# Delta-rule stage of a two-block kernel: gates' chain and small inverse in two parts, key tiles in banks 0 to 2, one gate for two head pairs

## Chip, cores, metric

One core of one Trainium2 chip runs the whole program in one launch. The metric is the device time in microseconds (us), the median of three runs. Six engines' queues matter: TensorE (PE; its weight loads are listed as PEld), VectorE (DVE), ScalarE (ACT), GpSimd (POOL, which only fills constants here), SyncE (SP), whose queue issues every DMA, and the DMA engines themselves. TensorE runs at one of two clocks, 1.2 or 2.4 GHz; the profile gives the granted clock as a share, 0.50 or 1.00.

## What is computed

A tensor x of 256 tokens by 1024 channels goes through a first block (convolution and pooling mixer, then a gated feed-forward part), and then through two layers: a gated delta rule, and a block attention, each with a layer norm and a SwiGLU feed-forward part. The change touches the delta rule alone, with 8 heads of 128 keys and 128 values, cut to what matters:

```python
proj = x @ w_in                                    # q, k, v, z, b, a
qkv = silu(causal_depthwise_conv(qkv, w_conv))     # 4 taps
q, k = l2_normalize(q) * 128 ** -0.5, l2_normalize(k)
beta = sigmoid(b)
g = -exp(a_log) * softplus(a + dt_bias)
gc = cumsum(g)                                     # within a chunk
low = strict_tril((k * beta) @ k.T * decay)        # decay = exp(gc_i - gc_j)
u, w = solve(I + low, [v * beta, k * beta * exp(gc)])
v_new = u - w @ state
o = (q * exp(gc)) @ state + tril(q @ k.T * decay) @ v_new
state = state * exp(gc_last) + k_dec.T @ v_new
o = o * rsqrt(mean(o * o) + eps) * norm_g * silu(z)
y = o @ w_out
```

The kernel works with two chunks of 128 tokens (index c) and handles the heads in halves (q = 0, 1: four heads) or in pairs (u = 0 to 3).

## The kernel before

**Matmuls.** Every product with a weight is made of three float32r matmuls, `three` (L489): high part of the weight by high and low part of the data, low part by high part. A weight unit is a 128 by 1024 block. ScalarE makes its high part (`high`, L962), VectorE its low part (`low`, L1422), four units ahead of TensorE.

**The order.** `delta_order` (L123) is written out by hand and called by TensorE, ScalarE and VectorE alike, each with its own functions; every engine runs its share in that order and waits on semaphores. A function named "nothing" means that the engine has no part in the step. Steps are:

- `tile(n)`: key tiles n = 0 to 7, value tiles 8 to 15, query tiles 16 to 23, 24 matmuls each on TensorE, in two halves. ScalarE then scales the last tap (L1210, out of the bank), VectorE adds three taps (L1732) and ScalarE's silu (L1200) follows in the next tile. Tiles use banks 4 to 6 in turn.
- `ba`, `gsum`, `rows`, `decays`: the gates. TensorE makes b and a (bank 7); ScalarE and VectorE make beta and g (L1159 to L1164, L1693 to L1703, ending in gg); TensorE sums g (`gsum`, L705); VectorE copies the sums (gcol, L1710); `rows(c, q)` (L715) spreads them along rows, ScalarE takes them out (L1172 and L1176 or L1179), VectorE caps them (L1716); `decays` takes exponentials (L1184 to L1195).
- `kturn(q)` turns four heads' keys (ScalarE squares them, L1217, takes a root, L1220, VectorE scales, L1748), `kback(q)` turns them back (ScalarE copies, L1227 and L1232), `kk(q)` multiplies keys by keys (L671; VectorE makes low of it in crow, L1767), `lowT(q)` turns low.
- `z(k)`: the eight z units, into all of banks 4 to 7; ScalarE's silu of them (L1154) is at k = 7.
- `inv(q)`: VectorE inverts the 16 by 16 blocks on the diagonal in 15 rounds (L1786, L1789). The blocks come and go by SP's DMAs: low out and in (L447, L451), the inverse out and back into tm (L454, L461). `turnT(q)` turns that, then `level_p` and `level_t` double the block size by products.
- `vturn`, `solve`, `state`, `carry`: values, the solve, the state between chunks.
- `qk(u)`, `attnT(u)`, `o(u)`, `gate(u)`, `gturn(u)`: attention within the chunk (L818), its turn (L833), the output (L841, L848), its norm with z (VectorE L1866 to L1877, ScalarE L1297 and L1300), its turn (L856). `qk(u)` also sums q squares (L824, squares from ScalarE, L1282, in crow).
- `gout(k)`: eight units of w_out.

**Banks.** Small steps take banks 0 to 3 in a ring (`Ring`, L110, `take_bank`): the fifth taker waits until the event that the first named has passed. Semaphores count, in each engine's own order.

Of the kernel before, what the change touches and what calls it, by code (L numbers as in the profile page):

```python
# [13 lines left out]
P = 128  # L14
# [108 lines left out]
def delta_order(do):  # L123
# [81 lines left out]
    do["gturn"](2)  # L205
    do["gout"](2)
    do["o"](3)
    do["gate"](3)
# [77 lines left out]
def program(nc, wts, head, vecs, csts, xtok, xT, low_dram, inv_dram, out):  # L286
    with ExitStack() as ctx:
# [90 lines left out]
        pba = bank[7][:, 0:32].rearrange("p (c n) -> p c n", c=2)  # L378
# [104 lines left out]
        def tensor(g, s):  # L483
# [178 lines left out]
            core_bank = Ring({b: ("hl", ("x2", 0)) for b in range(4)})  # L662
# [17 lines left out]
            def z(k):  # L680
# [1437 lines left out]
```

## Time and profile before

| | us |
|---|---|
| median of 3 runs | 1186.29 (1185.02 to 1186.57) |
| profiled execution, its own time | 1184.9 |
| its span, first to last instruction | 1183.1 |
| mean granted clock of TensorE | 0.982 |

The page of the profile gives the busy time of each engine as a share of the span, the chain of work that ended last, and the costliest groups of instructions. TensorE's busy time is an average over stages; in the delta-rule stage, from 422.6 to 643.9 us of the span, it is 196.12 of 221.3 us. A bracket at the end of a row of the timeline is the idle time of that engine before the row and the instruction that ended it. Matmuls overlap, so a row's start, not its duration, tells when the next could begin.

### The profile page before, as it was taken

Reading aid. Unit: us, or ns where it says so; the run is one execution under the profiler, and the core shown is the slowest. Engines: PE = TensorE matmul, PEld = TensorE weight load, DVE = VectorE, ACT = ScalarE, POOL = GpSimd, SP = SyncE. Lnnn points to the kernel's source line nnn. Section 1 sums busy time; section 2 is a strip of 40 time slices with the busy share of each in tenths; the row PEclk is TensorE's granted clock in tenths of the full one; section 3 lists DMA queues with packets and bytes.
Section 4 is the critical chain, followed back from the end, with each engine's and each line's share of the span. In section 5 each row is a group of like instructions: output and inputs, shape, how many; then the busy total and the mean of one; then the engine's idle time right before and its main releaser. Section 6 shows DMA issues by size and latency. Waiting matters only on the chain.

```text
span 1183.1 us, 21225 instructions
## 1 busy us (share of the span) xinstructions
PE 1124.9 (95%) x8872; PEld 1094.1 (92%) x8872; DVE 811.5 (69%) x1364; ACT 619.9 (52%) x1037; POOL 3.3 (0%) x13
## 2 busy tenths in 40 slices
PE   7998989999999996979989999999999999999998
PEld 7998878899999985879989999999999899999997
DVE  7987479878887776585666755555688557555554
ACT  5567454555466567633463554544455446544442
POOL 0000000000000000000000000000000000000000
PEclk9999999999999997989989999999999999999999
DMA  9985247267766512233223365656346335555500
GB/s 372 409 327 168 72 143 285 89 197 236 253 203 202 193 54 93 70 101 130 90 71 127 107 205 186 196 182 194 108 161 195 108 107 158 186 191 186 189 2 36
DMA packets 58127, 194.71 MB, mean 165 GB/s; under 512 B 10800, under 2 KB 11184, under 8 KB 57904
## 3 DMA queue, kind: packets, MB, share of 16 engines
q1 hardware_dynamic: 58032, 193.35, 48.9%
q8 instruction: 70, 1.15, 0.4%
q14 instruction: 25, 0.20, 0.1%
HBM read 192.02 MB, written 1.31 MB: 163 GB/s over the span
## 4 chain that ended last, share of the span: by engine, by line
PE 74%; DVE 17%; ACT 6%; issue 2%; SPq 1%; DMA 0%; POOL 0%; ACTq 0%; DVEq 0%; POOLq 0%
PE ps L492 61%; DVE lo L1422 4%; PE ps L671 3%; ACT hi L962 2%; PE ps L499 2%; DVE raw L1409 2%; PE ps L590 2%; DVE B L1431 1%; PE ps L511 1%; DVE st L1439 1%; DVE ev L1660 1%; DVE B L1444 1%; DVE B L1732 1%; PE ps L487 1%; DVE ev L1657 1%
## 5 line engine op out<-in xcount | busy, mean ns | idle before, releaser
L492 PE MATMUL ps<-hh,hi 128*128 128x256 f32 x1792 | 509.8, 285 | 15.6 <-DVE hl L1456 3.5
L492 PE MATMUL ps<-hl,hi 128*128 128x256 f32 x1792 | 503.2, 281 | 0.0
L492 PE MATMUL ps<-hh,lo 128*128 128x256 f32 x1792 | 503.0, 281 | 0.0
L1422 DVE TENSOR_TENSOR lo<-raw,hi 128x1024 fp32r<-128x1024 f32 x311 | 378.1, 1222 | 175.4 <-ACT hi L962 174.7
L492 PEld LDWEIGHTS ps<-hh,hi 128*128 128x128 f32 x1792 | 340.2, 190 | 19.3 <-issue 8.9
L962 ACT ACTIVATE hi<-raw 128x1024 fp32r<-128x1024 f32 x311 | 324.4, 1052 | 50.4 <-PE ps L492 50.3
L492 PEld LDWEIGHTS ps<-hl,hi 128*128 128x128 f32 x1792 | 340.1, 190 | 0.3
L492 PEld LDWEIGHTS ps<-hh,lo 128*128 128x128 f32 x1792 | 340.0, 190 | 0.0
L492 PE MATMUL ps<-fh,hi 128*128 128x256 f32 x568 | 159.4, 281 | 2.9 <-ACT B L1066 2.9
L492 PE MATMUL ps<-fh,lo 128*128 128x256 f32 x568 | 158.5, 279 | 0.0
L492 PE MATMUL ps<-fl,hi 128*128 128x256 f32 x568 | 158.4, 279 | 0.0
L492 PEld LDWEIGHTS ps<-fh,hi 128*128 128x128 f32 x568 | 106.8, 188 | 3.5 <-ACT B L1066 3.5
L492 PEld LDWEIGHTS ps<-fl,hi 128*128 128x128 f32 x568 | 106.8, 188 | 0.0
L492 PEld LDWEIGHTS ps<-fh,lo 128*128 128x128 f32 x568 | 106.8, 188 | 0.0
L1123 ACT ACTIVATE ev<-ps 128x256 f32<-128x256 f32 x88 | 33.7, 383 | 121.4 <-PE ps L492 121.4
L487 PE MATMUL ps<-idle 128*128 128x256 f32 x456 | 62.2, 294 | 1.7 <-POOL Z L477 1.7
L487 PEld LDWEIGHTS ps<-idle 128*128 128x128 f32 x456 | 58.4, 196 | 2.6 <-POOL Z L477 1.7
L1409 DVE CUSTOM_DVE_ANT_0 raw<-raw,crow 128x1024 f32<-128x1024 f32 x48 | 58.3, 1218 | 0.0
L1667 DVE TENSOR_TENSOR ev<-ev 128x256 f32<-128x256 f32 x66 | 28.0, 425 | 37.4 <-ACT ev L1123 26.8
L1669 DVE TENSOR_TENSOR fl<-ev,fh 128x256 fp32r<-128x256 f32 x66 | 28.1, 426 | 32.0 <-ACT fh L1127 32.0
L1732 DVE SCALAR_TENSOR_TENSOR B<-ps,vec,B 128x255 f32<-128x255 f32 (+2 forms) x72 | 34.6, 481 | 18.6 <-ACT B L1210 16.9
L1127 ACT ACTIVATE fh<-ev 128x256 fp32r<-128x256 f32 x66 | 27.6, 419 | 37.6 <-DVE ev L1667 37.6
(242 smaller groups left out, 1096.5 us busy)
## 6 DMA issues: line engine op xcount, KB each, us to landing
raw<-in_w SPq DMA_DIRECT2D x359, 512.0 KB, 4.1
B<-in_t SPq DMA_DIRECT2D x2, 512.0 KB, 5.5
xa<-in_x SPq DMA_DIRECT2D x1, 1024.0 KB, 11.6
out<-h SPq DMA_DIRECT2D x2, 512.0 KB, 2.9
cst<-in_c SPq DMA_DIRECT2D x1, 984.0 KB, 9.4
B<-between SPq DMA_DIRECT2D x32, 4.0 KB, 1.6
vec<-in_v SPq DMA_DIRECT2D x1, 328.5 KB, 7.3
between<-crow SPq DMA_DIRECT2D x16, 8.0 KB, 1.5
```

Of the source, the lines that this page charges most:

```text
L487: g.matmul(bank[7][:, 0:S], idle[:, 0:P], idle[:, :], start=True, stop=True, skip_group_check=True)
L492: m = g.matmul(o, l, r, start=first and n == 0, stop=last and n == 2, skip_group_check=True)
L499: m = g.matmul(bank[bm][:, 0:S], ones[:, one, :], y[:, k, :], start=k == 0, stop=k == nch - 1, skip_group_check=True)
L671: m = g.matmul(bank[b][:, i * P:i * P + P], left(i), right(i), start=i == 0, stop=True, skip_group_check=True)
L962: g.activation(hi[:, j % SPLIT, :], raw[:, PLACE[j] % RAW, :], ACT.Copy).then_inc(*up("hi", j))
L1123: g.activation(e, p, ACT.Copy if half else ACT.Silu).then_inc(*up("ff_out", (kup, t)))
L1127: g.activation(fh[:, j % 4, :], ev[:, (2 * j) % 4, :], ACT.Copy).then_inc(*up("f_hi", (kup, j)))
L1409: g.tensor_tensor_reduce(r, r, crow[:, :], 1.0, 0.0, ALU.mult, ALU.add, mod[:, col:col + 1]).then_inc(*up("ada", n))
L1422: g.tensor_tensor(lo[:, j % SPLIT, :], raw[:, PLACE[j] % RAW, :], hi[:, j % SPLIT, :].bitcast(F), ALU.subtract).then_inc(*up("lo", j))
L1667: g.tensor_tensor(e0, e0, e1, ALU.mult).then_inc(*up("f", (kup, j)))
L1669: g.tensor_tensor(fl[:, j % 4, :], e0, fh[:, j % 4, :].bitcast(F), ALU.subtract).then_inc(*up("f_lo", (kup, j)))
L1732: m = g.scalar_tensor_tensor(out=dst[:, d:], in0=bank[b][:, 0:S - d], scalar=V("a_conv", t * 4 + i), in1=dst[:, d:], op0=ALU.mult, op1=ALU ...
```

## The change

It writes `delta_order` in another way and adapts the functions to it:

1. Key tiles 0 to 7 use banks 0 to 2 (`tile_bank`), b and a and the sums bank 3, and rows(0, 0) and rows(0, 1) banks 6 and 7. z(0) waits for rows(0, 1) alone, and not for the last key tiles; the ring's banks wait for the last key tiles instead.
2. The gates' chain is in two parts, `soft(0)` after tile 3 and `soft(1)` after tile 4; gsum comes after tile 5, rows(0, 0) after tile 6, rows(0, 1) and kturn(0) after tile 7, rows(1, q) and decays after z(0), kback(0) after z(1).
3. inv(1) is in two parts, six rounds after tile 8 and nine after tile 9. ScalarE's silu of z takes the banks in the order 2, 0, 1, 3.
4. The q sums move from qk(u) to attnT(u), in bank 7 (a ring bank for u = 3).
5. gate(0) and gate(1) become one step with one root and one reciprocal, after tile 22; o, qk, attnT, gturn and gout are in another order from tile 19 on.

```diff
     for n in range(8):
         tile(n)
         if n == 2:
             do["ba"]()
+        elif n == 3:
+            do["soft"](0)
         elif n == 4:
+            do["soft"](1)
+        elif n == 5:
             do["gsum"]()
+        elif n == 6:
             do["rows"](0, 0)
+        elif n == 7:
             do["rows"](0, 1)
-        elif n == 5:
-            do["rows"](1, 0)
-            do["rows"](1, 1)
-        elif n == 6:
             do["kturn"](0)
     for k in range(8):
         do["z"](k)
         if k == 0:
+            do["rows"](1, 0)
+            do["rows"](1, 1)
             do["decays"]()
+        elif k == 1:
             do["kback"](0)
-        elif k == 1:
             do["kturn"](1)
...
         elif k == 6:
-            do["inv"](0)
+            do["inv"](0, 0, 15)
     tile(8)
-    do["inv"](1)
+    do["inv"](1, 0, 6)
     tile(9)
+    do["inv"](1, 6, 15)
...
-    tile(19, [then("qk", 0)], [then("attnT", 0), then("state", 1)])
-    tile(20, [then("o", 0), then("carry", 1)], [then("gate", 0)])
-    tile(21, [then("qk", 1), then("solve", 3)], [then("attnT", 1), then("gturn", 0)])
-    tile(22, [then("o", 1)], [then("gate", 1)])
-    tile(23, [then("qk", 2), then("gturn", 1)], [then("attnT", 2)])
+    tile(19, [then("qk", 0)], [then("state", 1)])
+    tile(20, [then("attnT", 0), then("carry", 1)], [then("qk", 1)])
+    tile(21, [then("o", 0), then("solve", 3)], [then("attnT", 1)])
+    tile(22, [then("o", 1)], [then("gate", 0, 1)])
+    tile(23, [then("qk", 2)], [then("gturn", 0), then("gturn", 1), then("attnT", 2)])
     do["last"]()
+    do["gout"](0)
+    do["qk"](3)
     do["o"](2)
-    do["gout"](0)
-    do["gate"](2)
-    do["qk"](3)
     do["gout"](1)
     do["attnT"](3)
-    do["gturn"](2)
+    do["gate"](2)
     do["gout"](2)
     do["o"](3)
+    do["gturn"](2)
     do["gate"](3)
...
+        def tile_bank(n):
+            return n % 3 if n < 8 else 4 + n % 3
...
-            core_bank = Ring({b: ("hl", ("x2", 0)) for b in range(4)})
+            core_bank = Ring({0: ("conv4", 6), 1: ("conv4", 7), 2: ("conv4", 5), 3: ("gcum", 0)})
...
                 if k == 0:
-                    for n in (5, 6, 7):
-                        s.wait_ge(*at("conv4", n))
-                    s.wait_ge(*at("gcum"))
+                    s.wait_ge(*at("rows_out", (0, 1)))
...
-                b = take_bank("rows_out", (c, q))
+                b = take_bank("rows_out", (c, q)) if c else 6 + q
...
+                b = take_bank("qss", 3) if u == 3 else 7
+                if u < 3:
+                    s.wait_ge(*(at("qss", u - 1) if u else at("z", 3)))
+                s.wait_ge(*at("qsq", u))
...
-                        [at("conv4", n) for n in (21, 22, 23)] + [at("z", 3)] if k == 0 else [])
+                        [at("conv4", n) for n in (21, 22, 23)] + [at("qss", 2)] if k == 0 else [])
...
-                    for b in range(4):
+                    for b in (2, 0, 1, 3):
```

The order of instructions shows what this does to the queues. First ScalarE from the tap of tile 2 on (sm holds the gates, hi a weight's high part, B keys; L1200 and L1159 to L1164 before are L1210 and L1168 to L1174 after). Before:

```order
L1210 ACTIVATE B<-ps,vec 128x256
L1159 ACT_TABLE_LOAD
L1159 ACTIVATE sm<-ps 128x16
L1160 ACT_TABLE_LOAD
L1160 ACTIVATE sm<-vec 128x8
L1162 ACTIVATE sm<-sm 128x16
L1164 ACT_TABLE_LOAD
L1164 ACTIVATE sm<-sm 128x16
L962 ACTIVATE hi<-raw 128x1024
```

Now, from the second operation of soft(0) on (the Exp of a_log):

```order
L1169 ACTIVATE sm<-vec 128x8
L1171 ACTIVATE sm<-sm 128x16
L970 ACTIVATE hi<-raw 128x1024
L1210 ACT_TABLE_LOAD
L1210 ACTIVATE B<-B 128x256
L1220 ACTIVATE B<-ps,vec 128x256
L1174 ACT_TABLE_LOAD
L1174 ACTIVATE sm<-sm 128x16
L970 ACTIVATE hi<-raw 128x1024
```

A high part, a Silu load, a silu and a tap stand between the two halves of the chain.

Second, ScalarE around z(0) and z(1) (Z holds rows and decays; the last two rows before are kback(0)'s copies). Before:

```order
L1200 ACTIVATE B<-B 128x256
L1184 ACT_TABLE_LOAD
L1184 ACTIVATE sm<-sm 128x16
L1186 ACTIVATE sm<-sm 128x8
L1191 ACTIVATE Z<-Z 128x512 x4
L1195 ACTIVATE Z<-Z 128x512 x2
L1227 ACTIVATE Z<-B,sm 128x128 x4
L1232 ACTIVATE B<-ps 128x4x128 x2
```

Now:

```order
L1189 ACTIVATE Z<-ps 128x512
L1194 ACT_TABLE_LOAD
L1194 ACTIVATE sm<-sm 128x16
L1196 ACTIVATE sm<-sm 128x8
L1201 ACTIVATE Z<-Z 128x512 x4
L1205 ACTIVATE Z<-Z 128x512 x2
L970 ACTIVATE hi<-raw 128x1024
L1237 ACTIVATE Z<-B,sm 128x128 x4
L1242 ACTIVATE B<-ps 128x4x128 x2
```

The rows of the second chunk now stand right ahead of the decays, and a high part between the decays and the copies.

Third, VectorE at the gate behind tile 22 (sm holds sums and factors, the products write og in B; the first row is the last tap of tile 22). Before, gate(1) alone:

```order
L1732 SCALAR_TENSOR_TENSOR B<-ps,vec,B 128x253
L1866 TENSOR_REDUCE sm<-B 128x2x2
L1869 SCALAR_TENSOR_TENSOR sm<-sm 128x2x2
L1872 RECIPROCAL sm<-sm 128x2x2
L1877 SCALAR_TENSOR_TENSOR B<-ps,sm,B 128x128 x4
L1422 TENSOR_TENSOR lo<-raw,hi 128x1024
```

Now, gate(0, 1):

```order
L1747 SCALAR_TENSOR_TENSOR B<-ps,vec,B 128x253
L1883 TENSOR_REDUCE sm<-B 128x2x2
L1886 SCALAR_TENSOR_TENSOR sm<-sm 128x2x2
L1883 TENSOR_REDUCE sm<-B 128x2x2
L1886 SCALAR_TENSOR_TENSOR sm<-sm 128x2x2
L1890 RECIPROCAL sm<-sm 128x2x4
L1896 SCALAR_TENSOR_TENSOR B<-ps,sm,B 128x128 x8
L1434 TENSOR_TENSOR lo<-raw,hi 128x1024
```

The products of both pairs stand behind both sums and one common reciprocal.

## Rows read from the trace of the kernel before

**Rows 1.** The page, busy time of each engine: us, share of the span, instructions.

```profile
PE 1124.9 (95%) x8872; PEld 1094.1 (92%) x8872; DVE 811.5 (69%) x1364; ACT 619.9 (52%) x1037; POOL 3.3 (0%) x13
```

**Rows 2.** Timeline, TensorE in the stage: start, us, engine, line, operation [idle before, releaser].

```profile
442.67 0.61 PE L705 MATMUL ps<-sm,cst 128*128 128x8 f32 x4 [1.16 <-DVE sm L1703]
449.48 3.78 PE L715 MATMUL ps<-cst,sm 128*128 128x128 f32 x16 [6.20 <-DVE sm L1710]
...
470.71 0.77 PE L492 MATMUL ps<-hi,hh 128*128 128x512 f32 x1 [5.71 <-DVE B L1732]
...
482.89 1.95 PE L671 MATMUL ps<-B 128*128 128x128 f32 x16
...
504.89 0.39 PE L492 MATMUL ps<-hh,hi 128*128 128x256 f32 x1 [1.66 <-ACT B L1154]
...
518.35 1.54 PE L677 MATMUL ps<-first,B 128*128 128x128 f32 x6 [4.70 <-DMA B<-between]
...
595.34 1.05 PE L824 MATMUL ps<-ones,crow 128*128 128x1 f32 x8 [2.32 <-ACT crow L1282]
...
608.43 1.87 PE L824 MATMUL ps<-ones,crow 128*128 128x1 f32 x8 [2.32 <-ACT crow L1282]
```

**Rows 3.** Stretches of the stage: us, PE busy (instructions), granted clock, DMA share, GB/s.

```profile
444.30:454.60 10.30, 5.12 (x24) 0.50 0.31 102
468.20:475.10 6.90, 4.39 (x11) 0.51 0.47 156
516.00:522.80 6.80, 4.45 (x21) 0.50 0.56 167
608.20:615.00 6.80, 6.57 (x31) 0.50 0.25 78
```

**Rows 4.** Timeline, ScalarE between tiles 2 and 4.

```profile
440.69 1.28 ACT L1164 ACT_TABLE_LOAD   x1
441.98 0.21 ACT L1164 ACTIVATE sm<-sm 128x16 f32<-128x16 f32 x1
442.10 1.04 ACT L962 ACTIVATE hi<-raw 128x1024 fp32r<-128x1024 f32 x1
...
444.45 0.42 ACT L1200 ACTIVATE B<-B 128x256 f32<-128x256 f32 x1
444.78 0.46 ACT L1210 ACTIVATE B<-ps,vec 128x256 f32<-128x256 f32 x1
```

**Rows 5.** Timeline, VectorE: the three taps of tile 2, and the copy gcol.

```profile
437.78 1.51 DVE L1732 SCALAR_TENSOR_TENSOR B<-ps,vec,B 128x255 f32<-128x255 f32 x3
...
449.26 0.17 DVE L1710 COPY sm<-ps 128x16 f32<-128x16 f32 x1
```

**Rows 6.** Timeline, ScalarE: rows(1, 0), decays, and kback(0)'s copies.

```profile
457.66 1.15 ACT L1172 ACTIVATE Z<-ps,sm 128x128 f32<-128x128 f32 x4 [0.42 <-PE ps L715]
...
472.54 2.17 ACT L1191 ACTIVATE Z<-Z 128x512 f32<-128x512 f32 x4
...
475.67 1.26 ACT L1227 ACTIVATE Z<-B,sm 128x128 f32<-128x128 f32 x4
476.83 1.06 ACT L1232 ACTIVATE B<-ps 128x512 f32<-128x512 f32 x2
```

**Rows 7.** Timeline, VectorE: both products into crow, inv(0)'s first row, the row behind it.

```profile
485.16 2.15 DVE L1767 SCALAR_TENSOR_TENSOR crow<-ps,sm,Z 128x128 f32<-128x128 f32 x8
...
494.22 2.16 DVE L1767 SCALAR_TENSOR_TENSOR crow<-ps,sm,Z 128x128 f32<-128x128 f32 x8 [1.84 <-DMA between<-crow]
...
500.44 0.28 DVE L1780 COPY blk<-cst 64x256 f32<-64x256 f32 x1
...
507.72 2.34 DVE L1422 TENSOR_TENSOR lo<-raw,hi 128x1024 fp32r<-128x1024 f32 x2
```

**Rows 8.** Timeline, VectorE at gate(0): the sum of squares and the four products.

```profile
592.71 0.68 DVE L1866 TENSOR_REDUCE sm<-B 128x4 f32<-128x512 f32 x1
...
594.07 1.12 DVE L1877 SCALAR_TENSOR_TENSOR B<-ps,sm,B 128x128 f32<-128x128 f32 x4
```

More of the change, by code:

```diff
@@ L820, in qk @@
                 m.then_inc(*up("qk", u))
-                b = take_bank("qss", u)
-                s.wait_ge(*at("qsq", u))
-                for n in range(4):
-                    m = g.matmul(bank[b][:, n:n + 1], qsq[:, u % 2, n % 2, n // 2 * P:n // 2 * P + P], ones[:, 2, 0:1],
-                                 start=n == 0, stop=True, skip_group_check=True)
-                m.then_inc(*up("qss_mm", u))
             def attnT(u):
@@ L834, in attnT @@
                 m.then_inc(*up("attnT_mm", u))
+                b = take_bank("qss", 3) if u == 3 else 7
+                if u < 3:
+                    s.wait_ge(*(at("qss", u - 1) if u else at("z", 3)))
+                s.wait_ge(*at("qsq", u))
+                for n in range(4):
+                    m = g.matmul(bank[b][:, n:n + 1], qsq[:, u % 2, n % 2, n // 2 * P:n // 2 * P + P], ones[:, 2, 0:1],
+                                 start=n == 0, stop=True, skip_group_check=True)
+                m.then_inc(*up("qss_mm", u))
             def o(u):
@@ L861, in gout @@
                 rows_in("gout", k, 4, xh[:, k, :], xl[:, k, :], at("gl", k // 2), k == 0, k == 7,
-                        [at("conv4", n) for n in (21, 22, 23)] + [at("z", 3)] if k == 0 else [])
+                        [at("conv4", n) for n in (21, 22, 23)] + [at("qss", 2)] if k == 0 else [])
             def nothing(*a):
                 pass
-            delta_order({"z": z, "ba": ba, "gsum": gsum, "rows": rows, "decays": nothing, "tile": gdn_tile, "kturn": kturn,
+            delta_order({"z": z, "ba": ba, "soft": nothing, "gsum": gsum, "rows": rows, "decays": nothing, "tile": gdn_tile, "kturn": kturn,
                          "kback": kback, "kk": kk, "lowT": lowT, "inv": nothing, "turnT": turnT, "level_p": level_p, "level_t": level_t, "vturn": vturn,
@@ L1293, in o, with gate @@
                 o_bank[u] = take_bank()
-            def gate(u):
-                s.wait_ge(*at("o_mm", u))
-                g.activation(two(tm, u), by_two(o_bank[u]), ACT.Square).then_inc(*up("osq", u))
-                v = mo[:, :, 2 * u:2 * u + 2]
-                s.wait_ge(*at("orms", u))
-                g.activation(v, v, ACT.Sqrt).then_inc(*up("osd", u))
+            def gate(*us):
+                for u in us:
+                    s.wait_ge(*at("o_mm", u))
+                    g.activation(two(tm, u), by_two(o_bank[u]), ACT.Square).then_inc(*up("osq", u))
+                v = mo[:, :, 2 * us[0]:2 * us[-1] + 2]
+                s.wait_ge(*at("orms", us[-1]))
+                g.activation(v, v, ACT.Sqrt).then_inc(*up("osd", us[-1]))
             def gturn(u):
@@ L1315, in nothing @@
                 pass
-            delta_order({"z": z, "ba": ba, "gsum": nothing, "rows": rows, "decays": decays, "tile": gdn_tile, "kturn": kturn,
+            delta_order({"z": z, "ba": nothing, "soft": soft, "gsum": nothing, "rows": rows, "decays": decays, "tile": gdn_tile, "kturn": kturn,
                          "kback": kback, "kk": kk, "lowT": lowT, "inv": nothing, "turnT": turnT, "level_p": level_p, "level_t": level_t, "vturn": vturn,
@@ L1727, in gdn_tile @@
                     return
[L1728 removed]
+                dst, b = (kb, vb, qb)[n // 8][:, n % 8, :], tile_bank(n)
                 s.wait_ge(*at("conv4_0", n))
@@ L1774, in lowT, with inv @@
                 take_bank()
-            def inv(q):
+            def inv(q, j0, j1):
                 a, x = bm[q]
-                g.tensor_copy(x, C("eye16")[0:64, :].rearrange("p (i j) -> p i j", i=16)).then_inc(*up("inv", (q, 0)))
-                s.wait_ge(s_blk[q], 16)
-                for j in range(15):
+                if j0 == 0:
+                    g.tensor_copy(x, C("eye16")[0:64, :].rearrange("p (i j) -> p i j", i=16)).then_inc(*up("inv", (q, 0)))
+                    s.wait_ge(s_blk[q], 16)
+                for j in range(j0, j1):
                     n = 15 - j
@@ L1894, in nothing @@
                 pass
-            delta_order({"z": z, "ba": ba, "gsum": gsum, "rows": rows, "decays": decays, "tile": gdn_tile, "kturn": kturn,
+            delta_order({"z": z, "ba": nothing, "soft": soft, "gsum": gsum, "rows": rows, "decays": decays, "tile": gdn_tile, "kturn": kturn,
                          "kback": kback, "kk": kk, "lowT": lowT, "inv": inv, "turnT": turnT, "level_p": level_p, "level_t": level_t, "vturn": one_bank,
```

116 lines of the change are left out of this document (62 added, 54 removed).

## The prediction, on record before the changed kernel ran

> **What bounds it.** I read the page first: TensorE is busy 95% of the span [rows 1], so time can only come from the moments in which it waits or runs slowly. Next I read TensorE's timeline through the delta-rule stage (422.6 to 643.9) and looked only at rows with a bracket, which give the idle time and its releaser. There are seven long ones [rows 2]: 1.16 and 6.20 us in the gates' chain (for VectorE's gg, then its copy gcol), 5.71 before z(0) (for the taps of tile 7, because z takes the tiles' banks), 1.66 before tile 8 (for the third z activation on ScalarE), 4.70 before turnT(0) (for the small inverse coming back by DMA), and twice 2.32 at the q sums (for ScalarE's square into crow). Together 24.1 us. Third, the busy time by stretch: in four stretches the granted clock is 0.50, the lower level (1.2 GHz), and they hold 5.12 + 4.39 + 4.45 + 6.57 = 20.5 us of TensorE work [rows 3]. At the upper level that work takes half as long, so 10.3 us are lost there. Each stretch begins some 2 to 3 us into a wait (two adjoining waits in the first) and ends 4 to 7 us after work resumes; the waits of 1.66 and the first 2.32 drew none. The stage thus holds 34 us to be had. Last I read ScalarE's and VectorE's timelines, to see what each wait becomes once the order changes.
>
> **The change, part by part.** I carry one clock, the profile's, and put each engine's queue through the new order. A key tile costs TensorE about 2.85 us: three tiles lie between 504.89 and 513.65, where the wait for turnT(0) begins [rows 2].
>
> *Gates' chain.* Until tile 3 nothing moves. VectorE ends tile 2's taps at 439.3 [rows 5] and ScalarE its silu of it at 439.7. Now ScalarE does: tile 3's tap 0.4, Sigmoid load and beta 1.5, Exp load with two exps 1.6, a weight's high part 0.95, Silu load and silu 1.7, tap 0.4, Ln load and Ln 1.5 [rows 4]. That is 8.1 us, to 447.8; two small VectorE operations later gg stands at 448.2, not at 442.6. TensorE has tile 5 as new cover and ends it at 444.3 (441.5, the start of the 1.16 wait [rows 2], plus 2.8). It waits 4.0 us there. Then gsum 0.5 and tile 6, to 451.6. Meanwhile ScalarE needs high part, Silu load, silu and tap (3.1 us, to 450.9), VectorE three taps and the copy of gcol (1.5 + 0.2 [rows 5]): gcol stands at 452.5, so rows(0,0) waits 0.9. Rows(0,0) 1.0 (it and rows(0,1) took 3.78 at the lower clock [rows 2], so 1.9 at the upper) and tile 7 take TensorE to 456.4; rows(0,1) and one turn cover 1.4 us of tile 7's tap and taps, and the second turn, in bank 1, waits 1.3 for them. z(0) starts at 459.5. The 4.0 us wait should draw the lower clock; part of that hides under the waits behind it, and I add 0.5 between 0 and 2.6 (half of the mean 5.13 us of [rows 3]). So 460.0 instead of 470.71 [rows 2]. Of these 10.7 us, 1.8 are only postponed, since rows(1,0) and rows(1,1), which ran ahead of z(0), now follow it: 8.9 us ahead.
>
> *What is late next: ScalarE.* It was ahead of TensorE; now it isn't. Its last square of the first key turn ends at 460.8. Behind it, without a pause, stand Sqrt load and root 1.6, high part 0.95, Silu load and silu 1.7, rows(1,0) and rows(1,1) at 1.6 each (four activations 1.15 and a copy of 0.5, half the pair in the last row), Exp load and two small exps 1.6, six decays 3.2 (four take 2.17), high part 0.95, the four scaled copies 1.2 and the pair of copies 1.0 [rows 6]: 15.3 us, to 476.1. kk(0) needs that pair. TensorE has z(0) to z(2) at 2.8 each (twelve matmuls of 512 columns, a key tile's 24 of 256), the rows 1.9 and two pairs of turns at 0.8 as cover and is there at 471.9: **a new wait of 4.2 us**. kk(0) at 476.1 instead of 482.89 [rows 2] leaves 6.8 us. From there the chain goes on: squares, Sqrt load, high part (3.6 us, ScalarE at 479.7), VectorE's low part 1.2 and the products into crow 2.15, which end at 483.2 instead of 487.3 [rows 7]. The second products start 6.9 us later in both, since they wait for the DMAs of the first [rows 7], and end at 492.3 instead of 496.4. inv(0) follows 4.1 us after that in the profile, partly at TensorE's pace of z(5); behind VectorE alone I make it 3.5. inv(0) starts at 495.8 instead of 500.44: 4.6 us ahead. inv(0)'s 7.3 us and the 10.6 us from its end (507.8) to turnT(0) at 518.35 stay as they are [rows 2, 7]. So **turnT(0) comes 4.5 us earlier**, at 513.8, after a wait of about 6 us instead of 4.7. Bounds: 8.9, if ScalarE's queue does not hold kk(0), and 2.5, if the lower clock takes 2.6 before z(0).
>
> *z's activations in another order* release tile 8 about 1.0 us sooner (two activations of 0.5). It saves nothing: turnT(0), 8.6 us behind, waits for the DMA anyway. *inv(1) in two parts*: 9 of its 15 rounds (4.2 of 7.3 us) now stand behind tile 9's low part and taps, 2.7 us. TensorE asks for it two tiles and ten products behind turnT(0), some 15 us (kk's pair of products takes 1.95 [rows 2]), and no wait stands there now; I cost the split at nothing, and that stretch is its cover. VectorE does the same work between inv(0) and the first level product, so that does not move either.
>
> *The q sums and the joint gate.* The q sums move behind attnT, so both 2.32 us waits go [rows 2]. But bank order matters: from o(0), the fourth bank taken after its own is qk(2)'s, and o(0)'s bank is released by the gated product, which now comes from gate(0,1) for both pairs. ScalarE can square only after tile 22's tap, VectorE does tile 22's taps 1.5, then two reductions of 0.68 [rows 8], each with a small sum behind it (0.9 together), root and reciprocal 0.5, four products 1.12 [rows 8]: from tile 22's end on TensorE to the release 5.4 us, of which half a tile covers 1.4. **qk(2) waits 4.0 us**. Every wait of that length in [rows 2] drew the lower clock, so 2.6 more. Then gout(0) needs qss(2) on VectorE behind tile 23's taps and two gl: 1.6 us. Sum 8.2, against 2 x 2.32 + 6.57 / 2 = 7.9 before [rows 2, 3]: 0.3 us worse. Bounds: 2.4 us better with no lower clock, 2 worse with it held through gout(0).
>
> *Table loads.* Each takes 1.28 us and the activation starts 0.02 us behind it [rows 4]. One more stands in the gates' chain (Silu between Exp and Ln), one Sqrt load fewer at the joint gate; both are in the sums. The Trainium skill, "ScalarE: Activation LUTs", section "Table sets: the hidden batching unit", speaks against the split: activations are to be batched by set, and "What ACT_TABLE_LOAD costs" puts a switch at 2.66 us with its drain. By that price the five switches up to gcol would cost 6.9 us more and the lead would be gone (my estimate); the trace does not agree, it shows 1.28 and no drain behind it, so the measurement decides, and as a rival (1186, no change) it keeps no chance.
>
> **Sum.** 4.5 - 0.3 = 4.2 us. The profiled execution took 1184.9 (span 1183.1), 1.4 below the median of the three runs, 1186.3. 1180.7 in its terms, **1182.0 us** in the median's. A measurement of this kernel can tell about 0.2%, 2.4 us, from no change.
>
> **Rivals.** *All of the lead is kept* (ScalarE's queue holds less than I say, and the joint gate draws no lower clock): 8.9 + 2.4 = 11.3 us, 1175. For it: over the span ScalarE is busy only 52% of the time [rows 1]. Against: those 15.3 us are a plain queue. *The lead is given back at the second inverse*: inv(1) ends 2.7 us later behind inv(0), and its DMAs share SP's queue with the weights; if they land so late that turnT(1) waits 2 us and the clock falls (2.6 more), 4.6 are gone: 1186.5, no change. Against: the 15 us of tiles and products between. *Slower, by the clock*: the new order has four long waits as before (4.0, 4.2, 6, 4.0) and six short ones (0.6 to 1.6) close behind them. The first stretch of [rows 3] shows two adjoining waits holding the lower clock for 10.3 us. If the short ones do that everywhere, half-clocked work doubles to 41 us, which costs 10.3 more: 1192. It decides from 13 us more of such work (6.6 us lost). Against: after the wait of 5.71 the clock was back within 4.4 us of work. *The change doesn't do what it says*: for the split inverse and z's order that is my forecast already; for the gates, gg comes 5.6 us later, only the cover grows.
>
> **Chances.** My forecast 0.58, with its own range 1178.5 to 1185.5, of which 0.50 lies below 1183.9; all kept 0.13; given back 0.18 (0.05 faster, 0.13 same); slower 0.11. Faster 0.68, same 0.21, slower 0.11. The range 1176.5 to 1186.5 leaves out about half of the first rival, the whole slower case and a little of the third.
>
> **What would show it.** Right: in the changed profile TensorE waits about 4 us for VectorE at gsum, 1 to 1.5 at the second key turn, 3 to 5 for ScalarE's copies at kk(0), about 6 for the DMA at turnT(0), 4 for VectorE at qk(2), 1 to 2 at gout(0), none for crow; z(0) starts near 460, turnT(0) near 514. Wrong: no wait at kk(0) (then the first rival), a wait at turnT(1) (the second), more than 33 us of work at 0.50 (the third).

## The result, and the profile after

The changed kernel takes 1179.15 us in the median of 12 runs (1176.67 to 1182.92), the kernel before, in 12 runs beside them, 1186.05 us (1182.84 to 1188.83). The ratio is 0.9949 with a 95% interval of 0.9935 to 0.9962: 6.0 us faster by the ratio, 4.5 to 7.7 (the two medians lie 6.9 apart). The forecast was 4.2 us and 1182.0; 1179.15 lies at the lower end of its range (1178.5 to 1185.5). The profiled execution took 1179.46 (span 1177.7), 5.4 less than that of before (1184.9).

The page's busy time, which answers to [rows 1]: the same 8,872 matmuls, 3.7 us less of TensorE, VectorE and ScalarE unchanged. So work has not gone; waits and slow stretches have.

```profile
PE 1121.2 (95%) x8872; PEld 1090.4 (93%) x8872; DVE 811.3 (69%) x1363; ACT 620.0 (53%) x1035; POOL 3.3 (0%) x13
```

TensorE's timeline in the stage, the rows with a bracket, as in [rows 2]. The stage starts 0.65 us later than before (first tile's second step at 426.41 against 425.76), so 0.65 is to be taken off when a start is held against one of before.

```profile
448.93 1.02 PE L711 MATMUL ps<-sm,cst 128*128 128x8 f32 x4 [3.96 <-DVE sm L1717]
...
461.29 0.65 PE L685 MATMUL ps<-first,B 128*128 128x128 f32 x4 [0.99 <-DVE B L1747]
...
477.31 2.05 PE L679 MATMUL ps<-B 128*128 128x128 f32 x16 [3.44 <-ACT B L1242]
...
484.10 0.66 PE L685 MATMUL ps<-first,crow 128*128 128x128 f32 x4 [1.07 <-DVE crow L1782]
...
500.33 0.39 PE L500 MATMUL ps<-hh,hi 128*128 128x256 f32 x1 [0.69 <-ACT B L1162]
...
514.74 1.97 PE L685 MATMUL ps<-first,B 128*128 128x128 f32 x8 [5.73 <-DMA B<-between]
...
602.76 2.08 PE L824 MATMUL ps<-B 128*128 128x128 f32 x8 [3.94 <-DVE B L1896]
...
611.11 0.36 PE L500 MATMUL ps<-fh,hi 128*128 128x256 f32 x1 [0.88 <-DVE sm L1870]
```

The waits of 6.20 (rows), 5.71 (z(0)) and twice 2.32 (crow) are gone. New are 3.44 at kk(0) and 3.94 at qk(2), the wait at gsum grew from 1.16 to 3.96, that at turnT(0) from 4.70 to 5.73. In sum (with a second wait of 0.37 behind that of 1.07) 24.1 us of waiting became 21.1, so waiting explains 3.0 us. Most of the rest is the clock, in the stretches that answer to [rows 3] (from the third column on: busy time and instructions of PE, PEld, VectorE, ScalarE and GpSimd, then clock, DMA share and GB/s):

```profile
448.40:455.20 6.80, 6.28 (x29) 6.28 (x30) 4.31 (x9) 4.42 (x7) 0.00 (x0) 0.50 0.29 94
513.20:520.00 6.80, 5.26 (x25) 5.27 (x26) 6.15 (x23) 2.92 (x5) 0.00 (x0) 0.50 0.43 114
602.00:608.80 6.80, 6.04 (x28) 6.04 (x29) 4.71 (x12) 3.46 (x6) 0.00 (x0) 0.50 0.23 78
```

Three stretches at 0.50 (1.2 GHz) instead of four, with 17.6 us of work instead of 20.5; half of the difference, 1.5 us, is gained. The new wait at kk(0) drew none: from 475.0 to 500.0 the clock is 1.00. Together that is 4.5 of the 4.7 us by which the stage is shorter in these two profiles (224.8 and 220.1 us, the sums of the two columns of the table below).

ScalarE's timeline between its last square of the first key turn and the copies that kk(0) needs. Nothing in between has a bracket: one queue of 15.1 us (462.6 to 477.7).

```profile
461.98 0.60 ACT L1227 ACTIVATE h<-ps 128x512 f32<-128x512 f32 x1 [0.21 <-PE ps L685]
...
471.44 2.18 ACT L1201 ACTIVATE Z<-Z 128x512 f32<-128x512 f32 x4
...
475.51 1.26 ACT L1237 ACTIVATE Z<-B,sm 128x128 f32<-128x128 f32 x4
476.68 1.06 ACT L1242 ACTIVATE B<-ps 128x512 f32<-128x512 f32 x2
```

VectorE's timeline from the second key turn to the first small inverse, and then that of SyncE's queue from its end on. The inverse ends at 504.2; its result goes out in one DMA and comes back in 16, which take 7.35 us to issue; turnT(0) follows 1.2 us behind the last.

```profile
480.59 1.29 DVE L1763 TENSOR_TENSOR B<-ps,sm 128x512 f32<-128x512 f32 x2
481.79 1.22 DVE L1434 TENSOR_TENSOR lo<-raw,hi 128x1024 fp32r<-128x1024 f32 x1
482.92 2.16 DVE L1782 SCALAR_TENSOR_TENSOR crow<-ps,sm,Z 128x128 f32<-128x128 f32 x8
...
491.08 2.16 DVE L1782 SCALAR_TENSOR_TENSOR crow<-ps,sm,Z 128x128 f32<-128x128 f32 x8 [2.46 <-DMA between<-crow]
...
495.72 1.23 DVE L1434 TENSOR_TENSOR lo<-raw,hi 128x1024 fp32r<-128x1024 f32 x1 [1.34 <-ACT hi L970]
496.86 0.28 DVE L1796 COPY blk<-cst 64x256 f32<-64x256 f32 x1
```

```profile
504.23 0.47 SPq L462 DMA_DIRECT2D between<-blk  x1
...
506.18 7.35 SPq L469 DMA_DIRECT2D B<-between  x16
```

### The profile page after: what moved, and what is told of

The parts are those of the page before. It is cut to its first block, busy times and chain, and to the rows that moved or that the text cites. A ratio compares the mean times of both kernels' runs of the same rounds, so it can differ in the third digit from the quotient of the medians.

```text
span 1177.7 us, 21218 instructions
## 1 busy us (share of the span) xinstructions
PE 1121.2 (95%) x8872; PEld 1090.4 (93%) x8872; DVE 811.3 (69%) x1363; ACT 620.0 (53%) x1035; POOL 3.3 (0%) x13
## 4 chain that ended last, share of the span: by engine, by line
PE 72%; DVE 17%; ACT 7%; issue 2%; DMA 1%; SPq 1%; ACTq 0%; DVEq 0%
PE ps L500 60%; DVE lo L1434 4%; PE ps L679 3%; ACT hi L970 2%; PE ps L507 2%; DVE raw L1421 2%; PE ps L598 2%; DVE B L1443 1%; PE ps L519 1%; DVE st L1451 1%; DVE ev L1672 1%; DVE B L1456 1%; DVE ev L1669 1%; DVE B L1747 1%; PE ps L685 1%
```

## The experiments

The kernels are compared by two stretches of the profiled execution, beside the runs. "To turnT(0)" is from the first tile's matmul behind its wait of 0.78 us to the first matmul of turnT(0); "to the end" goes on from there to the sums over B, eight matmuls behind a wait of about 0.33 us, in the norm behind the stage. The last column but one is the mean granted clock over all runs of that kernel (before: 0.981 to 0.982).

| kernel | to turnT(0), us | to the end, us | ratio to before | interval | clock | median, us |
|---|---|---|---|---|---|---|
| before | 92.59 | 132.19 | 1 | | 0.981 | 1184.8 to 1186.2 |
| changed | 88.33 | 131.73 | 0.9949 | 0.9935 to 0.9962 | 0.985 | 1179.15 |
| front_only | 88.34 | 134.72 | 0.9976 | 0.9965 to 0.9987 | 0.984 | 1182.85 |
| tail_only | 91.18 | 133.03 | 1.0003 | 0.9989 to 1.0017 | 0.979 | 1186.72 |
| split_gate | 89.45 | 129.95 | 0.9952 | 0.9935 to 0.997 | 0.982 | 1179.22 |
| whole_gates | 86.01 | 132.83 | 0.9945 | 0.9926 to 0.9963 | 0.984 | 1178.41 |
| undo_small | 88.46 | 131.62 | 0.9971 | 0.9953 to 0.999 | 0.984 | 1182.01 |
| copies_first | 90.31 | 129.92 | 0.9974 | 0.9956 to 0.9992 | 0.983 | 1181.47 |
| lead | 88.27 | 138.90 | 1.0033 | 1.0016 to 1.005 | 0.983 | 1189.1 |
| late_gate | 88.51 | 125.93 | 0.9912 | 0.9886 to 0.9937 | 0.987 | 1175.92 |
| act_dma | 86.79 | 132.03 | 0.9953 | 0.9937 to 0.9969 | 0.985 | 1179.21 |
| early_late | 85.25 | 126.48 | 0.9891 | 0.9867 to 0.9915 | 0.990 | 1171.8 |
| best | 86.01 | 127.34 | 0.9886 | 0.9863 to 0.9909 | 0.989 | 1171.25 |
| best_gates | 85.54 | 127.58 | 0.9904 | 0.988 to 0.9927 | 0.987 | 1174.11 |

Behind each row stands one profile, and the same code does not give the same figure twice. The front of the changed kernel measures 88.33 to 89.45 us in four of them (changed, `front_only`, `split_gate`, `late_gate`), its tail 129.92 to 132.83 in five (changed, `whole_gates`, `undo_small`, `copies_first`, `act_dma`). A difference of about 1 us in the first column, or 3 us in the second, shows nothing by itself.

### The front alone, and the tail alone

`front_only` is the changed kernel with the lines of the order from tile 19 on, and the code of the q sums and gates, as before; `tail_only` is the kernel before with these of the changed one.

```diff
-    tile(20, [then("attnT", 0), then("carry", 1)], [then("qk", 1)])
-    tile(21, [then("o", 0), then("solve", 3)], [then("attnT", 1)])
-    tile(22, [then("o", 1)], [then("gate", 0, 1)])
+    tile(20, [then("o", 0), then("carry", 1)], [then("gate", 0)])
+    tile(21, [then("qk", 1), then("solve", 3)], [then("attnT", 1), then("gturn", 0)])
+    tile(22, [then("o", 1)], [then("gate", 1)])
...
```

> The changed kernel with the tail of the delta stage (q sums, gates of the heads, from tile 19 on) as it was before. Theory A (the prediction's sum): the gain comes from the first half, through the lead at turnT(0); the time is 4 to 5 us below the kernel before (ratio about 0.996), both waits of 2.32 us for the square into crow are back, turnT(0) starts within 0.5 us of the changed kernel's 514.74. Rival B: the tail made the gain (q sums moved) and the lead at turnT(0) is eaten behind it; then this one is within 2.4 us of the kernel before.

> The kernel before with only the tail of the changed one (q sums behind attnT, one gate for two pairs). Theory A: no wait for crow, but a wait of about 4 us at qk(2) for the gated product with the lower clock behind it; sum within 1.5 us of the kernel before (ratio 0.999 to 1.001). Rival B: the q sums carry the gain, 3 us or more below before (ratio 0.997 or less). Rival C: the wait at qk(2) costs more than what went, 2 us or more above before.

The front alone gains 2.8 us (1.5 to 4.2), the tail alone nothing (1.3 faster to 2.0 slower). Theory A holds for the tail; for the front, A asked for 4 to 5, which only the top of the interval reaches, while the lead at turnT(0) is there in full (88.34 against 88.33). The two do not add up to the 6.0 of the change: on top of the front the tail is worth about 3.2 us (1.2 to 5.2, from 0.9949 / 0.9976), on top of the kernel before nothing. The profiles point to the clock. TensorE's waits for crow in `front_only`, and the stretches behind them:

```profile
593.29 1.87 PE L830 MATMUL ps<-ones,crow 128*128 128x1 f32 x8 [2.32 <-ACT crow L1290]
...
609.49 1.27 PE L830 MATMUL ps<-ones,crow 128*128 128x1 f32 x8 [2.32 <-ACT crow L1290]
```

```profile
593.10:599.90 6.80, 6.61 (x31) 6.62 (x32) 2.94 (x6) 2.07 (x4) 0.00 (x0) 0.50 0.22 77
610.10:613.50 3.40, 3.40 (x18) 3.40 (x19) 2.13 (x5) 1.72 (x2) 0.00 (x0) 0.51 0.47 157
```

The same two waits drew the lower clock once in the profile of before (6.57 us of work) and twice here (10.0). In `tail_only` the wait of 3.94 at qk(2) stands as in the changed kernel, two stretches follow it (8.3 us of work instead of 6.04), and the mean clock over all runs is the lowest of the table:

```profile
606.50:613.30 6.80, 4.94 (x23) 4.94 (x24) 4.68 (x13) 3.64 (x6) 0.00 (x0) 0.50 0.26 72
616.70:620.10 3.40, 3.37 (x16) 3.40 (x17) 1.22 (x1) 0.48 (x1) 0.00 (x0) 0.50 0.36 96
```

One profile for each is no proof, and why the waits draw more in one order than in the other stays open. No run takes the parts of the front (the banks, the later rows and sums) one from another; what each is worth by itself isn't known.

### The joint gate apart

> The changed kernel, but gate(0) behind tile 21 and gate(1) behind tile 22, each by itself; the q sums stay behind attnT. Theory A: the wait of 3.94 us at qk(2) is made by the joint gate, since o(0)'s bank is released by a product that now comes with gate(1). Apart, the wait goes, and with it the stretch at the lower clock behind it (6.04 us of work, 3.0 lost): 4 to 7 us below the changed kernel (1172 to 1175). Rival: one more Sqrt load and one more Silu load (1.28 us each) delay ScalarE's taps, and the wait moves to tile 22 or to gout(0) at 2 to 4 us: within 2.4 us of the changed kernel.

```diff
-    tile(21, [then("o", 0), then("solve", 3)], [then("attnT", 1)])
-    tile(22, [then("o", 1)], [then("gate", 0, 1)])
+    tile(21, [then("o", 0), then("solve", 3)], [then("attnT", 1), then("gate", 0)])
+    tile(22, [then("o", 1)], [then("gate", 1)])
```

The rival came true. The wait at qk(2) is gone, and three others hold most of it (3.8 us instead of the 4.8 at qk(2) and gout(0)); the ratio, 0.9952, is that of the changed kernel. The profile is of the longest of its seven runs (1183.72). TensorE's rows, then all engines from tile 21's end to gout(0) (columns as above):

```profile
606.86 0.66 PE L864 MATMUL ps<-first,B 128*128 128x128 f32 x4 [0.60 <-DVE B L1896]
...
608.59 0.66 PE L833 MATMUL ps<-first,Z 128*128 128x128 f32 x4 [1.08 <-DVE Z L1860]
...
612.18 0.55 PE L500 MATMUL ps<-fh,hi 128*128 128x256 f32 x1 [2.11 <-DVE sm L1870]
```

```profile
597.00:612.20 15.20, 11.41 (x98) 10.89 (x96) 13.34 (x32) 14.43 (x23) 0.00 (x0) 0.92 0.26 87
```

VectorE is busy 13.3 of 15.2 us and ScalarE 14.4, TensorE 11.4. That points to the two engines' load as the cause, with the bank only naming the place; `late_gate`, below, tests it.

### The gates' chain in one part

> The changed kernel, but the gates' chain undivided behind tile 2 as before (one table load fewer), while gsum stays behind tile 5. Theory A: the cover of one more tile is what helps, and the split works against it, since it puts a high part, a silu and a tap between Exp and Ln; undivided, gg stands near 443.5 instead of 448.9, the wait of 3.96 us at gsum goes, and with it the stretch at the lower clock (6.28 us of work, 3.1 lost): z(0) starts 4 us earlier or more, the time is 3 to 7 us below the changed kernel. Rival: the undivided chain holds ScalarE's taps of tiles 3 to 5 back, TensorE waits for these instead, and the lead at kk(0) stays ScalarE's: within 2.4 us of the changed kernel.

```diff
             do["ba"]()
-        elif n == 3:
             do["soft"](0)
-        elif n == 4:
             do["soft"](1)
```

gsum no longer waits, but tile 6 does, for the taps of tile 3, whose bank it takes, as the rival had it (TensorE's timeline):

```profile
446.30 0.39 PE L498 MATMUL ps<-hh,hi 128*128 128x256 f32 x1 [2.18 <-DVE B L1745]
...
473.79 1.62 PE L677 MATMUL ps<-B 128*128 128x128 f32 x9 [3.44 <-ACT B L1240]
```

turnT(0) comes 2.3 us earlier in the profile, but the tail, with the same code, takes 1.1 more (8.88 us of work at the lower clock in it instead of 6.04), and the time is 0.5 us below the changed kernel by the ratios, which these runs cannot tell from nothing. The wait at kk(0) is 3.44 as in the changed kernel: its place moves with ScalarE's queue, its length doesn't.

### The two small parts undone

> The changed kernel with two of its parts undone together: z's four activations in the order 0, 1, 2, 3 again, and the second small inverse in one part behind tile 8. Theory A (the prediction): both are worth nothing, since the wait for the DMA at turnT(0) follows whichever comes first; time within 2 us of the changed kernel's 1179, the wait before tile 8 about 1.7 instead of 0.69 us, turnT(0)'s wait shorter by as much, turnT(0) at the same place behind the first tile. Rival: the undivided inverse holds VectorE 2.7 us longer ahead of tile 9's low part and taps, TensorE runs dry behind turnT(0): 2.4 us or more above the changed kernel.

```diff
-    do["inv"](1, 0, 6)
+    do["inv"](1, 0, 15)
     tile(9)
-    do["inv"](1, 6, 15)
...
-                    for b in (2, 0, 1, 3):
+                    for b in range(4):
```

In TensorE's timeline theory A is right to 0.2 us: the wait before tile 8 is 1.66 again, that at turnT(0) shorter by 0.91, and both stretches of the table stay.

```profile
501.30 0.39 PE L499 MATMUL ps<-hh,hi 128*128 128x256 f32 x1 [1.66 <-ACT B L1161]
...
514.88 1.54 PE L684 MATMUL ps<-first,B 128*128 128x128 f32 x6 [4.82 <-DMA B<-between]
```

Nor does TensorE wait anywhere for 0.3 us or more between turnT(0) and qk(2), as the rival had it. But this is the profile of a run of 1179.42, and the median of the twelve is 1182.01. By the ratios (0.9971, interval 0.9953 to 0.999, against 0.9949) the two parts are worth 2.6 us, with an error that reaches from nothing to some 5, and the rival's 2.4 lies within it. The profile thus shows them worth nothing in one execution; the runs leave it open.

### kk(0)'s copies first

> The changed kernel, but on ScalarE the pair of copies that kk(0) needs goes ahead of the four scaled copies, of the decays of the second head group and of the two exps of qdec (3.4 us of other work). Theory A: the wait of 3.44 us at kk(0) is ScalarE's queue and nothing else, so it falls to 0 to 1 us; but the products that build the small matrix stand behind the second key turn on VectorE, and ScalarE's work up to that turn's root is as long as before, so the small inverse and turnT(0) do not come earlier: the wait for the DMA grows by 2.5 to 3.5 us (to 8 or 9), and the time is within 2.4 us of the changed kernel. Rival: kk(0) is the head of the chain, then turnT(0) comes 3 us earlier with it, and the time falls 3 us or more.

The edit is on ScalarE alone; `rest` holds the decays of the second head group and qdec's exps:

```diff
             def kback(q):
+                for c in range(2):
+                    b = take_bank()
+                    s.wait_ge(*at("kback_mm", (c, q)))
+                    g.activation(kb[:, 4 * q:4 * q + 4, c * P:c * P + P], quad(b), ACT.Copy).then_inc(*up("kback", (c, q)))
+                if q == 0:
+                    rest()
                 s.wait_ge(*at("kdec"))
...
```

TensorE's timeline:

```profile
474.38 2.05 PE L679 MATMUL ps<-B 128*128 128x128 f32 x16 [0.20 <-ACT B L1241]
481.66 1.25 PE L685 MATMUL ps<-first,B 128*128 128x128 f32 x8 [2.43 <-DVE B L1770]
484.43 2.15 PE L685 MATMUL ps<-first,crow 128*128 128x128 f32 x8 [1.51 <-DVE crow L1789]
```

Theory A again: the wait at kk(0) falls from 3.44 to 0.20 and the time does not follow; by the ratios it is 3.0 us above the changed kernel's (0.3 to 5.6), where A had it within 2.4. VectorE starts its first products into crow at 483.25, 56.6 us behind the first tile, and at 56.5 (482.92 less 426.41) in the changed kernel: they stand behind the second key turn. One figure of theory A missed: the wait at turnT(0) is 5.74 and not 8 or 9, since turnT(0) comes 2.0 us later and TensorE with it. The waits of 2.43 and 1.51 above were followed by the lower clock (0.50 from 482.9 to 489.7), VectorE's second products stood 2.32 us behind TensorE's kk(1), and the inverse starts 72.4 us behind the first tile instead of 70.5. A wait that is not on the chain only moves, and what it becomes has its own price.

### The chain itself in another order

> The same copies first, and the chain behind them shortened as well: kk(0) ahead of the second key turn on every engine, the first small inverse on VectorE ahead of the second pair of products (its DMAs on SyncE's queue placed to match), lowT(1) behind tile 8, turnT(1) behind tile 13. Theory A: the lead is set by the chain kk(0), products into crow, small inverse, DMAs, turnT(0): it starts some 7 us earlier, turnT(0) comes up to 9 us earlier and its wait of 5.73 falls under 2; with the wait at kk(0) gone too and fewer stretches at the lower clock, 8 to 12 us below the changed kernel (1167 to 1171). Rival: the second product pair and the second inverse now come later, and TensorE waits for them at lowT(1) or turnT(1): within 2.4 us of the changed kernel.

```diff
-DELTA_AT = {23: ("low", 0), 0: ("blk", 0), 1: ("low", 1), 2: ("blk", 1), 3: ("inv", 0), 4: ("tm", 0), 5: ("inv", 1),
+DELTA_AT = {23: ("low", 0), 0: ("blk", 0), 1: ("inv", 0), 2: ("low", 1), 3: ("tm", 0), 4: ("blk", 1), 5: ("inv", 1),
...
             do["kback"](0)
-            do["kturn"](1)
         elif k == 2:
             do["kk"](0)
+            do["kturn"](1)
         elif k == 3:
-            do["kback"](1)
             do["lowT"](0)
         elif k == 4:
-            do["kk"](1)
-        elif k == 5:
-            do["lowT"](1)
-        elif k == 6:
+            do["kback"](1)
             do["inv"](0, 0, 15)
+        elif k == 5:
+            do["kk"](1)
     tile(8)
+    do["lowT"](1)
...
```

(Beside this, ScalarE's edit of `copies_first`, inv(1) and turnT(1) a tile later.) This failed, 3.9 us slower than before. The inverse did run 6.0 us earlier (its first product at 492.48, 64.8 us behind the first tile, instead of 70.8), but its DMAs back stand on SyncE's queue behind the 8 of the second product pair, and the second inverse's input (L458) stands behind these 16: it is issued at 515.13 only, so VectorE stands still for 8.15 us and TensorE for 6.42 behind it. Theory A and the rival both missed; the rival had seen that the second inverse comes late, not that SyncE's queue makes it so, and 2.4 us were far too few. SyncE's queue, VectorE, TensorE:

```profile
499.47 0.46 SPq L461 DMA_DIRECT2D between<-blk  x1
...
502.72 3.91 SPq L454 DMA_DIRECT2D between<-crow  x8
...
507.22 7.40 SPq L468 DMA_DIRECT2D B<-between  x16
...
515.13 0.47 SPq L458 DMA_DIRECT2D ev<-between  x1
```

```profile
518.38 0.17 DVE L1808 TENSOR_TENSOR ev<-ev,blk 64x15 f32<-64x15 f32 x1 [8.15 <-DMA ev<-between]
```

```profile
515.95 1.97 PE L684 MATMUL ps<-first,B 128*128 128x128 f32 x8 [6.98 <-DMA B<-between]
...
529.65 2.05 PE L678 MATMUL ps<-ev,B 128*128 128x128 f32 x8 [6.42 <-DVE ev L1827]
```

### The second gate later

> The changed kernel with another tail: gate(0) behind tile 21, gate(1) only behind tile 23 (its result is not needed before gout(2)), gturn(0) and attnT(2) ahead of it. In the run with the gates merely apart TensorE's waits moved to 0.60, 1.08 and 2.11 us behind tile 22, because VectorE was full from 597 to 612. Theory A: the tail is bound by VectorE's queue there, so only taking 2.2 us of gate(1) out of it helps: waits from qk(2) to gout(0) sum to under 2 us instead of 4.8, with the clock held 3 to 5 us below the changed kernel (1174 to 1176). Rival: the tail's length is the chain tile 23, taps, gout(0), whatever stands between; within 2.4 us.

```diff
-    tile(22, [then("o", 1)], [then("gate", 0, 1)])
-    tile(23, [then("qk", 2)], [then("gturn", 0), then("gturn", 1), then("attnT", 2)])
+    tile(22, [then("o", 1)], [then("gturn", 0)])
+    tile(23, [then("qk", 2)], [then("attnT", 2)])
     do["last"]()
+    do["gate"](1)
     do["gout"](0)
     do["qk"](3)
+    do["gturn"](1)
```

(Beside this, gate(0) behind tile 21.) Three waits of 0.52 to 0.58 are left, and from 521.0 to 641.7 the clock is 1.00. The stretch that answers to that of `split_gate`:

```profile
597.00:612.00 15.00, 13.32 (x113) 12.87 (x112) 12.29 (x25) 11.04 (x18) 0.00 (x0) 1.00 0.28 97
```

The tail takes 125.93 us instead of 131.73, less than any of the five profiles of the changed tail, and the time is 1175.92, 4.4 us below the changed kernel by the ratios: the tail is bound by VectorE and ScalarE, and what needn't be there yet belongs behind it. The intervals of this and the changed kernel (0.9886 to 0.9937, 0.9935 to 0.9962) just touch.

### The small inverse: its DMAs, its start, and both

> The changed kernel, but of the 16 small DMAs that bring the first small inverse back, 8 are issued from ScalarE's queue (between the two halves of tile 10) and 8 from SyncE's, where all 16 took 7.35 us to issue, one behind the other. Theory A: the wait of 5.73 us at turnT(0) is for the most part the issuing of these 16, so turnT(0) comes 3 to 4 us earlier, its wait falls to 2 or 3 us, and with the shorter wait the stretch at the lower clock behind it goes in part: 3 to 6 us below the changed kernel. Rival: the DMAs themselves (landing 1.6 us each) or the weights on the same rings set the wait, so two queues issue no faster in sum; or ScalarE, blocked until the inverse is out, holds tile 10's tap back; within 2 us of the changed kernel.

> The changed kernel with the later gate(1) of the run before (waits from qk(2) to gout(0) summed to 1.7 us there) and with the first small inverse on VectorE one key step earlier, behind z(5)'s low part instead of z(6)'s (in the changed kernel VectorE waited 1.34 us for a high part and spent 1.2 on it ahead of the inverse, whose input had landed). Theory A: turnT(0) comes 2 to 2.5 us earlier and its wait falls to about 3.3 us; beside the tail's gain 5 to 8 us below the changed kernel in all (1171 to 1174). Rival: VectorE's low parts of the next tiles come 7 us later and TensorE waits for them ahead of tile 9: then no more than the tail's gain, 1175 to 1177.

> Both of these together: the earlier inverse, its DMAs back on two queues, and the later gate(1). Theory A: the wait at turnT(0) goes (5.73 less 2.5 less 3.5), and the lower clock behind it; the changed kernel less 3.5 for the tail, less 5.7, less 2 to 3 for the clock: 1166 to 1170. Rival: with the DMAs' wait gone TensorE arrives earlier at tiles 11 and 12 and waits for VectorE, which is now behind: 1171 to 1176.

```diff
+            def tm_in():
+                s.wait_ge(s_inv[0], 16)
+                s.wait_ge(*at("fill", "tm"))
+                for b in range(8):
+                    d = slice(16 * b, 16 * b + 16)
+                    g.dma_start(tm[d, 2, :, d], inv_dram[0, 4:8, b].rearrange("n i j -> i n j")).then_inc(s_tm[0], 16)
...
         elif k == 5:
             do["lowT"](1)
-        elif k == 6:
             do["inv"](0, 0, 15)
```

In `act_dma` theory A falls. The issues are as fast as hoped, 8 in 3.6 us on either queue, but ScalarE's begin 1.8 us behind SyncE's, the wait at turnT(0) is shorter by 0.9 only, and the ratio is that of the changed kernel. In `best` and `best_gates`, which have the same edit, they begin 3.0 us behind SyncE's (506.21 against 503.21, 508.38 against 505.43). In all three runs they begin 0.1 to 0.3 us behind the silu of tile 9, which stands behind them in the program and waits for VectorE's taps. What held the second queue isn't known. The timelines of SyncE's and ScalarE's queues, then TensorE's:

```profile
506.55 3.62 SPq L469 DMA_DIRECT2D B<-between  x8
```

```profile
508.36 0.36 ACTq L1259 DMA_DIRECT2D B<-between  x1
...
509.22 2.83 ACTq L1259 DMA_DIRECT2D B<-between  x6
```

```profile
514.22 1.97 PE L685 MATMUL ps<-first,B 128*128 128x128 f32 x8 [4.85 <-DMA B<-between]
```

In `early_late` the inverse starts behind z(5)'s low part (at 495.22, 67.4 us behind the first tile instead of 70.5) and turnT(0) waits 3.19 instead of 5.73; with the later gate it is 1171.8, as theory A said. The profile shows this gain; the runs alone do not tell `early_late` from `late_gate` (0.9891 and 0.9912, with intervals that overlap). `best` has both, and there theory A missed: the wait is 2.60 and not gone, 1171.25 is the rival's figure, and the second queue adds nothing that can be told. VectorE's row of the inverse in `early_late`, then TensorE's rows of `early_late` and of `best`:

```profile
495.22 0.28 DVE L1797 COPY blk<-cst 64x256 f32<-64x256 f32 x1
```

```profile
513.10 1.45 PE L686 MATMUL ps<-first,B 128*128 128x128 f32 x8 [3.19 <-DMA B<-between]
```

```profile
511.51 1.09 PE L686 MATMUL ps<-first,B 128*128 128x128 f32 x8 [2.60 <-DMA B<-between]
```

> The version with the later gate(1), the earlier inverse and its DMAs on two queues, and the gates' chain undivided behind tile 3 (not split over tiles 3 and 4, nor whole behind tile 2, where it held tile 3's tap back by 2.18 us). Theory A: Ln follows Exp without a high part, a silu and a tap between, gg stands near 446 instead of 448.9, the wait at gsum falls from 3.96 to about 1 us, and all that hangs on ScalarE's queue behind it (kk(0), the inverse, turnT(0)) comes 2 to 3 us earlier: 2 to 5 us below the version without it (1166 to 1169, ratio 0.984 to 0.987). Rival: the tap of tile 4 comes late by the chain's length and tile 7, which takes its bank, waits for it as tile 6 did for tile 3's: within 2 us of the version without it (ratio 0.987 to 0.990).

`best_gates` takes out one line (`elif n == 4:`), so that the whole chain stands behind tile 3. The wait at gsum falls to 0.92, as theory A said, and the next one takes its place: gcol, on VectorE behind two tiles' low parts and taps, comes late for rows(0,0). The rival's wait at tile 7 does not show either; still there is no gain over `best`, as the rival said, and 1174.11 is above what either text gave (TensorE's timeline):

```profile
447.51 0.61 PE L711 MATMUL ps<-sm,cst 128*128 128x8 f32 x4 [0.92 <-DVE sm L1724]
454.32 2.07 PE L721 MATMUL ps<-cst,sm 128*128 128x128 f32 x8 [3.28 <-DVE sm L1731]
```

The shortest of all are `early_late` and `best`, 13 us below the kernel before (10 to 16) and clearly below the changed one.

## Why the prediction was right

The waits that I forecast came, at their places and nearly at their lengths, and none of my signs of being wrong showed: kk(0) waits, turnT(1) doesn't, and 17.6 us of the stage's work ran at 0.50, not 33. That the sum came so near the time is in part luck, as the paragraph on the tail says.

*The gates' chain.* The wait at gsum is 3.96 for 4.0, at the second key turn 0.99 for 1.3. The predicted wait of 0.9 at rows(0,0) did not show, since tile 6 ran at the lower clock and took its time: the stretch of 448.4 to 455.2 holds 6.28 us of work, 3.1 lost, of which I had costed 0.5. That cost and the waits that fell away nearly cancel: z(0) starts behind the second key turn at 461.7, by before's clock 461.0 for 460.0.

*ScalarE is late next.* The queue is 15.1 us for 15.3, kk(0) starts at 476.7 (477.31 less 0.65) for 476.1, its wait is 3.44 for 4.2. Here one step was left out: between the root and the products into crow VectorE also scales the second key turn (two operations, 1.29, L1763), so these products end at 484.4 for 483.2. A second error took that back: the second products start 6.0 us behind the end of the first (485.08, 491.08), not the 6.9 that I took from before, and end at 492.6 for 492.3. The waits of 1.07 and 0.37 for crow behind kk(0) are in no term of my sum; the wait at turnT(0) takes them in. My text put kk(0) itself on the chain ("from there the chain goes on"); `copies_first` shows that it isn't. ScalarE's queue up to the second root and VectorE's behind it are.

*turnT(0)* comes 4.26 us earlier for 4.5 and waits 5.73 for 6; turnT(1) waits for nothing, and the rival of the second inverse fell. *z's order* and *inv(1) in two parts* are worth nothing by the profile of `undo_small`, while its runs leave up to some 5 us open.

*The tail* is the term that was mis-sized, "0.3 us worse". The new waits were right (3.94 for 4.0 at qk(2), 0.88 for 1.6 at gout(0), 3.0 lost to the clock for 2.6), and by itself the tail is indeed worth nothing. But I had put what it removes at 7.9 us from a single execution. `front_only`'s profile shows the same waits for crow drawing 10.0 us of work at the lower clock instead of 6.57, and on top of the front the tail is worth some 3.2 us. As far as one profile for each can show it, this is what the forecast lacks, 4.2 against 6.0. By the profiles of before and after alone the parts came out as forecast: 4.26 us for 4.5 up to turnT(0), and 0.46 behind it (132.19 less 131.73) for -0.3. By the runs they did not: the front gives 2.8 (1.5 to 4.2) for 4.5, the tail on top of it 3.2 (1.2 to 5.2) for -0.3, and the two misses partly cancel in the sum.

*Table loads.* Each takes 1.28 us, and Ln starts at 448.24 for a load that began at 446.94; nothing like a drain stands behind one. `whole_gates` saves one load and moves the wait only.

*Two slips of arithmetic* changed nothing: the three tiles between 504.89 and 513.65 take 2.92 us each, not 2.85, and 4.2 below 1186.3 is 1182.1.

## What to carry to other kernels

Before a wait is removed, ask whose queue is full there: at qk(2) the bank named the place, but only taking VectorE's and ScalarE's work out of the stretch (`late_gate`) brought time, not putting it elsewhere within it (`split_gate`). A chain through several engines is as long as its longest queue; a queue of small DMA issues counted here with 0.46 us for each (16 in 7.35). Before a DMA is moved on such a queue, see what stands behind it (`lead`). Time at the lower clock behind a wait has to be read from several executions before it enters a sum: the same tail took 129.92 to 132.83 us in five of them.

## What the runs showed of the hardware

Runs of one kernel differ with the granted clock: of the changed kernel's 12 the fastest has a mean clock of 0.989 and 1176.67 us, the slowest 0.978 and 1182.92. A wait of about 4 us at gsum was followed by 6.28 us of work at the lower clock; the wait of 3.44 at kk(0) by none in the changed kernel, and by 3.50 in `whole_gates` (474.50 to 478.00, at 0.51). ScalarE's small DMAs began 1.8 us behind SyncE's in `act_dma` and 3.0 in `best` and `best_gates`, although both waited for the same signal, and an activation that stands behind them in the program started ahead of the first in all three (by 0.07 us in `act_dma`, at 508.29).
